# A seven-product form of the X projection in the state-space stage of a two-block float32 network on one TensorE

## The reference, cut to what matters

```
h, hc = modulated rms_norm of x and of the context        # 256 x 2048 each
xbc   = silu(dw_conv5(h  @ w_in[:, X|B|C]))               # X 2048, B 1024, C 1024 columns
xbc_c = silu(dw_conv5(hc @ w_in[:, X|B|C]))               # the context needs X and B
dt    = softplus(h @ w_in[:, dt] + dt_bias)               # 64 columns, sequence and context
y     = forward scan + backward scan over two chunks of 128 tokens, started from the context's state
yb    = gated_group_rmsnorm(y + d * X, z)                 # z = h @ w_in[:, Z]
out   = concat(ya, yb) @ w_out                            # ya is the attention's result
```

## Time and profile before

| | |
|---|---|
| median of 3 runs | 2744.59 us |
| profiled execution, its own time | 2744.42 us |
| span of its profile | 2742.2 us |
| TensorE busy | 2697.4 us, 98% |
| VectorE busy | 1608.3 us, 59% |
| ScalarE busy | 470.3 us, 17% |
| mean granted TensorE clock | 0.994 |
| HBM traffic | 450.18 MB, 164 GB/s |

### The profile page before, as it was taken

How to read it: one execution, slowest core, us unless ns; L and a number is a source line. 1 busy time by engine, 2 the same in 40 slices (tenths; PEclk the granted TensorE clock), 3 DMA queues, 4 the chain that set the end, 5 groups by cost and what they waited for, 6 DMA issues and landing times.

```text
span 2742.2 us, 45093 instructions
## 1 busy us (share of the span) xinstructions
PE 2697.4 (98%) x19040; PEld 2349.0 (86%) x19040; DVE 1608.3 (59%) x2801; ACT 470.3 (17%) x925; POOL 51.2 (2%) x72
## 2 busy tenths in 40 slices
PE   6999999999999999999999999999999999999999
PEld 1399999999997666666668998999999999999999
DVE  3677766777674255555555536666666654555543
ACT  0221212121111122222221001111111111122211
POOL 0000000000000000000000000000000000000000
PEclk9999999999999999999999999999999999999999
DMA  9855755576455333333334555555555454455542
GB/s 387 299 170 189 240 182 177 179 231 208 151 181 195 123 108 108 107 98 93 92 100 138 185 175 155 162 174 163 169 167 174 138 164 143 150 158 157 160 132 84
DMA packets 380522, 450.18 MB, mean 164 GB/s; under 512 B 20452, under 2 KB 351704, under 8 KB 379480
## 3 DMA queue, kind: packets, MB, share of 16 engines
q1 hardware_dynamic: 351232, 354.86, 41.7%
q0 software_dynamic: 19520, 75.50, 7.7%
q10 hardware_dynamic: 9624, 17.68, 1.7%
HBM read 441.66 MB, written 6.36 MB: 163 GB/s over the span
## 4 chain that ended last, share of the span: by engine, by line
PE 98%; DMA 1%; DVE 0%; ACT 0%; issue 0%; SPq 0%; DVEq 0%; ACTq 0%
PE bank L563 91%; PE wide L563 5%; DMA w<-in_ada_w 1%; PE wide L566 1%; PE bank L566 0%; DVE xT L1772 0%; DVE yT L1773 0%; ACT work L1250 0%; DVE ssq L2178 0%; DMA cs_rows<-work 0%; ACT hT L1250 0%; ACT rs L1250 0%; DVE yT L2112 0%; DVE hT L2265 0%; DVE hT L1799 0%
## 5 line engine op out<-in xcount | busy, mean ns | idle before, releaser
L563 PE MATMUL bank<-hT,w 128*128 128x128 f32 (+2 forms) x6464 | 1048.7, 321 | 9.2 <-ACT hT L1250 4.6
L563 PEld LDWEIGHTS bank<-hT,w 128*128 128x128 f32 x6464 | 830.3, 193 | 192.5 <-issue 179.2
L563 PE MATMUL bank<-yT,w 128*128 128x128 f32 (+1 forms) x3552 | 475.3, 294 | 1.0 <-DVE yT L2112 1.0
L563 PEld LDWEIGHTS bank<-yT,w 128*128 128x128 f32 x3552 | 451.4, 192 | 17.2 <-DVE yT L2112 1.2
L1250 ACT ACTIVATE work<-bank 128x512 f32<-128x512 f32 (+2 forms) x308 | 159.1, 525 | 1292.9 <-PE bank L563 1239.8
L563 PE MATMUL bank<-hT,work 128*128 128x128 f32 x2672 | 316.9, 276 | 0.0
L563 PEld LDWEIGHTS bank<-hT,work 128*128 128x128 f32 x2672 | 307.5, 192 | 0.0
L563 PEld LDWEIGHTS bank<-w,hT 128*128 128x128 f32 x1792 | 245.2, 192 | 19.2 <-issue 5.7
L563 PE MATMUL bank<-w,hT 128*128 128x128 f32 (+2 forms) x1792 | 261.4, 305 | 0.0
L1250 ACT ACTIVATE work<-work 128x512 f32<-128x512 f32 (+3 forms) x299 | 168.5, 569 | 291.9 <-DVE work L2009 150.8
L1854 DVE SCALAR_TENSOR_TENSOR work<-xT,silc,work 128x512 f32<-128x512 f32 x240 | 180.3, 751 | 34.5 <-DMA xT<-in_ada_w 27.7
(11 more groups left out here) (204 smaller groups left out, 2228.2 us busy)
## 6 DMA issues: line engine op xcount, KB each, us to landing
w<-in_na_ssd_w_in SPq DMA_DIRECT2D x48, 2048.0 KB, 11.1
xT<-in_ada_w POOLq DMA_DIRECT2D x64, 1024.0 KB, 8.5
w<-in_sc_w_in SPq DMA_DIRECT2D x32, 2048.0 KB, 9.3
w<-in_w_in SPq DMA_DIRECT2D x32, 2048.0 KB, 9.3
w<-in_na_ssd_w_out SPq DMA_DIRECT2D x16, 2048.0 KB, 9.6
w<-in_ada_w SPq DMA_DIRECT2D x12, 2048.0 KB, 12.1
w<-in_na_ssd_w_in SPq DMA_DIRECT2D x16, 1024.0 KB, 8.8
w<-in_sc_w_out SPq DMA_DIRECT2D x8, 2048.0 KB, 8.3
```

The source lines that it names most:

```text
L563: return nc.tensor.matmul(dst, lhsT, rhs, start=start, stop=stop, skip_group_check=free)
```

## The change: what it does

X of group g > 0 is computed by seven products of 256 columns. The weights of a group are cut in four quarters (8 chunks deep, 128 columns wide), `hT` in four quarters too (8 chunks deep; sequence or context). VectorE forms t1, t2, t4 (into `xT`) and one sum in place (`x_weights`), each 128 x 1024, in every group; the sums of tokens are formed once, in group 0 (`token_sums(XC, ...)`, 128 x 2048 each, into all of `yT`). The seven results lie in four bank fills; ScalarE copies the first, VectorE adds the others (`x_first`, `x_second`, `x_third`) and writes the sums into `pad`. The convolutions of X therefore start later in the group. B's products stand in one piece.

`yT` and `xT` are taken, so a group's result goes to a small tile `yfeat` and from there to DRAM (`feature_store`, 256 KB on ScalarE's queue), and SP brings back x, the attention's result and the groups' results at the beginning of `out`. The last group's result is written into `yT` directly. Group 0 keeps the direct form of X.

The dt chain of group 0 is cut into pieces: `log_of_dt`, `sums_of_dt`, `rows_of_dt` on ScalarE, and the same on TensorE and VectorE, with convolutions and products between them. ScalarE takes both X halves out of PSUM ahead of them.

```diff
-    PHASES = [..., ("ssd", 8, 6, [2, 4, 6, 6]), ...
+    PHASES = [..., ("ssd", 8, 8, [4, 6, 8, 8]), ...
+    XC = lambda a, k: hT[:, EIGHT * k:EIGHT * (k + 1), a * T:(a + 1) * T]
+    XC_SUM = {j: yT[:, EIGHT * n:EIGHT * (n + 1), :] for n, j in enumerate((1, 2, 3, 4))}
+    x_staged = rs ...; x_partial = ssq ...
 SP, ssd(i):
-            if is_first(i): (reads of xT and yT)
 SP, out_proj(i), first pass:
+   s == 0, behind the load: y_scratch -> yT[0:16]; wait f_saved 16 * 6; f_scratch -> yT[16:28]
+   s == 1, behind the load: x_scratch -> xT
+   s == 2, behind the load: wait f_saved 16 * 7; f_scratch -> yT[28:30]
 TensorE:
+        def ssd_x(g, part):
+            dst = accumulate("ssd", part, g)
+            t1, t2, t4 = (x_places[:, m, :, :] for m in range(3))
+            a, b = dst[:, 0:T], dst[:, T:2 * T]
+            if part == 0:
+                pe.wait_ge(s_made, 12)
+                product(a, quarter(0, 0, 1), XC(0, 0))
+                last = product(b, quarter(0, 1, 1), XC(0, 1))
+            elif part == 1:
+                pe.wait_ge(x_t, 3 * g - 1)
+                product(a, t2, XC_SUM[2])
+                last = product(b, quarter(0, 0, 0), XC_SUM[3])
+            elif part == 2:
+                product(a, t1, XC_SUM[1])
+                ssd_within(g - 1, 1)
+                last = product(b, quarter(0, 1, 0), XC_SUM[4])
+            else:
+                pe.wait_ge(x_t, 3 * g)
+                last = product(a, t4, XC(1, 1))
 TensorE, ssd(g), g > 0:
-   X half 0; C*B; X half 1; states; within 0; B first half; within 1; across; within 2; B second half; within 3; C; z
+   x 0; C*B; x 1; states; within 0; x 2 (within 1 inside); within 2; x 3; across; within 3; B; C; z
 TensorE, g == 0:
-   B; sums_of_dt (with the transposes); C; z
+   B; sums_of_dt; C; rows_of_dt (the transposes); z
 ScalarE, ssd(g):
-   conv_in 0; (ssd_dt | ssd_scan); conv_in 1; states; conv_exp 0; conv_exp 1; conv_in 2; rms; conv_exp 2; conv_in 3; ...
+   g == 0: conv_in 0; conv_in 1; log_of_dt; conv_exp 0, 1; conv_in 2; sums_of_dt; conv_exp 2; conv_in 3; rows_of_dt; ...
+   g > 0:  staging_x; ssd_scan; states; conv_exp 0, 1; conv_in 2; rms; conv_exp 2; conv_in 3; ...; cs_rows; feature_store
 VectorE, ssd(g):
-   conv 0; (steps_of_dt | to_the_end, mask_cb, all_heads); conv 1; conv_silu 0; combine; conv_silu 1; ...
+   g == 0: conv 0; steps_of_dt; conv 1; logs_of_dt; conv_silu 0; token_sums(XC); conv_silu 1; conv 2; ends_of_dt; ...
+   g > 0:  x_weights; to_the_end; mask_cb; all_heads (x_first inside); x_second; conv 0; x_third; conv 1; conv_silu 0; combine; ...
+        def x_weights(g, link):
+            dve.wait_ge(w_loaded[0], loads(0, "ssd", g))
+            link(v.tensor_tensor(t1, quarter(0, 0, 0), quarter(0, 0, 1), ALU.subtract))
+            v.tensor_tensor(t2, quarter(0, 1, 0), t1, ALU.subtract).then_inc(x_t, 1)
+            v.tensor_tensor(quarter(0, 0, 0), quarter(0, 1, 0), quarter(0, 0, 0), ALU.subtract).then_inc(x_t, 1)
+            v.tensor_tensor(t4, quarter(0, 1, 1), t2, ALU.subtract).then_inc(x_t, 1)
+   x_first: 3 adds of 256 columns; x_second: one of 512, one of 256; x_third: one of 256
```

More of the change, by code:

```diff
@@ L1492, in ssd @@
             conv_in(g, 3)
+            if first:
+                rows_of_dt()
             conv_exp(g, 3)
@@ L1505, in ssd @@
             cs_rows(g)
+            if not first:
+                feature_store(g - 1)
         ssd_setup()
@@ L2085, in all_heads, with x_first, x_second, x_third @@
                 weights(s, r - 1, link)
+                if beside and r == 2:
+                    beside()
             weights(s, 3, link)
+        def x_weights(g, link):
+            t1, t2, t4 = (x_places[:, m, :, :] for m in range(3))
+            dve.wait_ge(w_loaded[0], loads(0, "ssd", g))
+            link(v.tensor_tensor(t1, quarter(0, 0, 0), quarter(0, 0, 1), ALU.subtract))
+            v.tensor_tensor(t2, quarter(0, 1, 0), t1, ALU.subtract).then_inc(x_t, 1)
+            v.tensor_tensor(quarter(0, 0, 0), quarter(0, 1, 0), quarter(0, 0, 0), ALU.subtract).then_inc(x_t, 1)
+            dve.wait_ge(x_t, 3 * g - 2)
+            v.tensor_tensor(t4, quarter(0, 1, 1), t2, ALU.subtract).then_inc(x_t, 1)
+        def x_first(g, link):
+            k = BANKS["ssd"] + 8 * g
+            dve.wait_ge(acc_free, k + 1)
+            dve.wait_ge(acc_full, k + 2)
+            v.tensor_tensor(x_partial[:, 0, :], x_staged[:, 0, :], bank[1][:, 0:T], ALU.add)
+            link(v.tensor_tensor(pad[:, 1, 0, 2:T + 2], x_staged[:, 0, :], x_staged[:, 1, :], ALU.add))
+            v.tensor_tensor(x_partial[:, 1, :], x_partial[:, 0, :], bank[1][:, T:2 * T], ALU.add).then_inc(acc_free, 1)
+            dve.wait_ge(acc_free, k + 2)
+        def x_second(g, link):
+            k = BANKS["ssd"] + 8 * g
+            dve.wait_ge(acc_full, k + 3)
+            link(v.tensor_tensor(pad[:, 0, :, 2:T + 2], x_partial, bank[0][:, 0:T].unsqueeze(1).broadcast_to([P, 2, T]), ALU.add))
+            v.tensor_tensor(pad[:, 0, 0, 2:T + 2], pad[:, 0, 0, 2:T + 2], bank[0][:, T:2 * T], ALU.add).then_inc(acc_free, 1)
+        def x_third(g):
+            k = BANKS["ssd"] + 8 * g
+            dve.wait_ge(acc_full, k + 4)
+            v.tensor_tensor(pad[:, 1, 1, 2:T + 2], x_partial[:, 1, :], bank[1][:, 0:T], ALU.add).then_inc(acc_free, 1)
         def combine(s, link):
@@ L2110, in features @@
             dve.wait_ge(s_ft, s + 1)
+            last = isinstance(s, int) and s == 7
+            if not last:
+                wait(dve, f_saved, 16 * s)
             for c in range(2):
-                v.tensor_scalar(chunk(yT, DC + 2 * s + c), bank[3][:, c * T:(c + 1) * T], col("ssd_norm_g", 2 * s + c),
-                                None, ALU.mult).then_inc(s_y, 1)
+                v.tensor_scalar(chunk(yT, DC + 2 * s + c) if last else yfeat[:, c, :], bank[3][:, c * T:(c + 1) * T],
+                                col("ssd_norm_g", 2 * s + c), None, ALU.mult).then_inc(s_y, 1)
         def ssd(g, link):
@@ L2117, in ssd @@
             s = g - 1
-            conv(g, 0, link)
             if first:
+                conv(g, 0, link)
                 steps_of_dt()
             else:
+                x_weights(g, link)
                 to_the_end(s)
                 mask_cb(s, link)
-                all_heads(s, link)
+                all_heads(s, link, lambda: x_first(g, link))
+                x_second(g, link)
+                conv(g, 0, link)
+                x_third(g)
             conv(g, 1, link)
+            if first:
+                logs_of_dt()
             conv_silu(g, 0, link)
-            if not first:
+            if first:
+                token_sums(XC, XC_SUM, (0, EIGHT), link)
+            else:
                 combine(s, link)
```

126 lines of the change are left out of this document (81 added, 45 removed).

## The result

The changed kernel takes 2716.65 us (2714.01 to 2719.12 in four runs) against 2744.74 before in the same comparison: a ratio of 0.9896, 95% interval 0.9883 to 0.9908. In a second comparison it was 2713.95 (2713.47 to 2716.55), ratio 0.9889 (0.9873 to 0.9906). The forecast was 2716.0. The profiled execution took 2714.01, with a span of 2711.8 against 2742.2; for it the forecast was 2715.8.

What follows compares the result with a forecast made beforehand. TensorE, busy 98% of the span, was taken as the bound; 22.4 us from X in seven groups plus 6.2 from group 0's dt chain make 28.6, taking the median 2744.59 to 2716.0, range 2713.0 to 2722.5.

Steps and rivals of the forecast that it cites:

- Bound: Whole kernel: TensorE, busy 98% of the span, sets the time; changes are summed on it alone unless something makes it wait.
- X by seven products: TensorE, seven groups: X 24.33 us instead of 27.46; with B and C 3.2 per group, 22.4 in all (bounds 21.7 to 23.9).
- The dt chain: Group 0 on TensorE: C follows the sums without standing, z starts 6.2 us sooner, 3.8 waiting and 2.4 clock.
- What VectorE must do in time: Each group, T its start on TensorE: X's weight sums done T + 5.5, needed T + 7.8; slack 2.3 us, no wait.
- Stores and reads: Groups and tail: stores and late reads cost 0; last decay sums 0 to 7 us late as bound.
- rival A: Tail: backlog of loads makes the last decay sums or slot 2 late by 1 to 7 us, 2717 to 2723; chance 0.07.
- B: Rival, group 0: the wait moves to another link and its 6.2 us stay, 2722.2; chance 0.05.
- C: Rival, each group: VectorE's sums d late cost 7 x (d - 2.3), slower than before from d = 6.4 us; chance 0.04.
- D: Rival, X on TensorE: weight loads stand in line with products at 0.192 us each, 2864 us; chance 0.01.

Runs made afterwards that it cites:

- x_direct: Changed kernel with X of all groups by the direct 512-column form in the old order, cut dt chain and stores kept: 2738.33 us, ratio to before 0.9975.
- chain_whole: Changed kernel with group 0's dt chain back in one piece on all engines, second X half taken out of PSUM behind it: 2721.66 us.
- rows_at_once: Changed kernel with only TensorE's two transposes of the dt sums put back right behind the sums in group 0: 2717.62 us.
- vector_late_1: Changed kernel with one extra 1024-column subtraction on VectorE (1.2 us) ahead of the sums of X's weights in every group: 2715.94 us.
- vector_late_4: Changed kernel with four extra 1024-column subtractions on VectorE (about 5.0 us) ahead of those sums in every group: 2741.46 us, ratio to before 0.9989.
- x_in_128: Changed kernel with each of X's seven products run as two of 128 columns, 224 weight loads a group for 112: 2723.62 us, ratio to before 0.9916.
- vector_late_6: Changed kernel with six extra 1024-column subtractions on VectorE (about 7.5 us) ahead of those sums in every group: 2769.33 us, ratio to before 1.0088.

## Why the prediction was right, point by point

**Bound.** TensorE's own stream set the time before and after, 98% of the span both times, and the sum on TensorE alone held.

**How close, and how much of it is luck.** The median came out 0.65 us from the forecast, and that is luck: the four executions are two near 2714 and two near 2719, and the second comparison gave 2713.95. The profile against its own forecast is the fairer test: 2714.01 against 2715.8. Of these 1.8 us, 0.6 are X, 0.3 the dt chain, and most of the rest the clock between `out` and the second layer, which I had not forecast.

**X by seven products.** Forecast 24.33 us a group, measured 24.34. I had rounded 3.25 down to 3.2; it is 3.29, which is 0.6 us over seven groups. `x_direct` gives 23.2 to 23.6 for the part alone. Of my bounds, 23.9 should have been 24.0 by its own rows (7 x (27.46 - 24.15 + 0.12)), which changes nothing. The price from a row of the smaller size was right; by columns alone it would have been 24.03, 2.2 us too little over seven groups.

**The dt chain.** Forecast 6.2, measured 6.5 in the timeline and 6.5 to 6.8 in `chain_whole`. The two sizes that were off: C starts 2.60 us after the start of the small products, not 2.76, because the length of a row holds a modelled end, and the transposes cost 0.22 beside a product, not 0.41. The split into waiting and clock is shown from both sides: `chain_whole` has the stand and the clock of 0.73, `rows_at_once` a wait of 0.7 and full clock.

**What VectorE must do in time.** T + 5.5 forecast, T + 5.3 measured, against T + 7.8; first head's weights T + 13 forecast, T + 13.5 measured. `vector_late_1` and `vector_late_4` enclose the slack: 1.2 us more is free, 5.0 more makes waits of 2.44.

**Stores and reads.** No cost that shows in the groups, by `x_direct`. The backlog that rival A feared had mostly cleared in time: the read of x landed 12.7 us after its issue, 2 us before the last group's end, where my bound had it 7 us behind that end. Left to chance is the last read of decay sums: against before, the states' products came 0.3 us late in the first profile of the changed kernel, not at all in the second, and 1.0 late in `x_in_128`. The last is the low end of rival A's 1 to 7.

**Rivals.** B was wrong: C and z follow without a wait. C did not happen, but it exists as a mechanism once VectorE is made late, and my price for it was too low: I set 7 x (d - 2.3), and `vector_late_6`, with d = 7.5, cost 51.1 where that gives 36.4. I had priced the waits and left out the clock behind them, though the earlier trace rows showed it and I had used it in group 0. With it, four late subtractions (24.1) take most of the gain of 30.4. Drawn straight between 24.1 at 5.0 us and 51.1 at 7.5, an estimate, the gain is gone near 5.6 us of lateness, not at 6.4. D is wrong by `x_in_128`: the loads are recorded at 0.19 us each, yet 64 of them with their products take 7.14 us, so a weight load of the whole array hides behind products that fill the whole array. The Trainium skill, "TensorE: Matmul & The Clock Gate", section "The mechanism", says in the line that the prediction used that a load overlaps only when its row groups differ; the runs disagree with that line. The opening paragraph of the same section also lets a load into "the background weight buffer" go ahead, which would allow what the runs show; no run here shows which buffer was used.

## What to carry to other kernels

Price a form with fewer columns by a row of the smaller size, and put the sums that it needs into an idle stretch that the profile shows; what then matters is the one slack, between the end of the sums and the product that asks for them. Look in a stream that is otherwise full for places where TensorE stands still for some microseconds: such a place costs its own length and what the low clock behind it takes (3.8 and 2.4 us here), and an earlier copy out of PSUM may end it. Where changes of a few microseconds are to be told apart, compare profiles from a mark behind the start.

## What the runs showed of the hardware that was not expected

- Waits of 2.44 to 2.53 us of TensorE lowered its clock in three of seven like places and not in the other four; waits of 5.0 did so in seven of seven, at some 2.0 us each; the products behind waits of 1.65 and 0.70 had the full clock (1.00).
- The clock can fall with no wait in front: over 48 instructions of two columns it was 0.94 in one profile and 0.65 in another, 5.8 and 8.1 us for the same work. With the rise at the start this moves all that follows by up to 4.6 us between executions of the same work (marks at 910.1 to 914.7).
- The sum of squares between `out` and the second layer, behind a wait of 2.03 to 2.04 us, took 1.13, 1.58, 1.59, 1.72, 2.03 or 2.08 us in different profiles.
- 128-column instructions run at 0.112 us each with a load apiece; the whole cost of doubling the loads is 0.8 us in 24.3.
